# Staggering the addresses of a kernel's weight slots and operand arrays modulo 512 bytes

## What is computed

```python
h = layer_norm(ALPHA * h + y, ln_g[i, 0], ln_b[i, 0])       # y: the mixer's output
u = jnp.square(jax.nn.relu(h @ w_up[i])) @ w_down[i]        # 1024 -> 4096 -> 1024
h = layer_norm(ALPHA * h + u, ln_g[i, 1], ln_b[i, 1])
h = h + jax.nn.sigmoid(h @ w_ple_gate[i]) * (p[i] @ w_ple[i])
```

## Time and profile before

| | |
|---|---|
| median of three runs | 3551.2 us |
| span of the profiled execution | 3552.2 us |
| matmuls | 18416 |
| of these 512 columns wide, lines 497 to 499 | 11328 |
| of these 256 columns wide, lines 530 to 532 and 618 to 620 | 4704 |
| TensorE (PE) busy | 99% |
| VectorE (DVE) / ScalarE (ACT) / GpSimd (POOL) busy | 50% / 27% / 18% |
| mean granted TensorE clock | 0.998 |

### The profile page before, as it was taken

The page is one execution under the profiler, slowest core; times in us unless marked ns, Lnnn a source line. Parts: engine busy times, 40 slices in busy tenths (PEclk is TensorE's granted clock), DMA queues, the critical chain, the costliest instruction groups (busy, mean ns, idle before and its releaser), DMA issues.

```text
span 3552.2 us, 44299 instructions
## 1 busy us (share of the span) xinstructions
PE 3512.9 (99%) x18416; PEld 2952.0 (83%) x18416; DVE 1766.9 (50%) x2276; ACT 960.4 (27%) x1679; POOL 632.3 (18%) x372
## 2 busy tenths in 40 slices
PE   9999999999999999999999999999999999999999
PEld 7788888889888888688888878888888888898887
DVE  5454334556653346763336445553474346563434
ACT  3562001334220013630013256210141215120102
POOL 2112111200131112031112111311121111211110
PEclk9999999999999999999999999999999999999999
DMA  5322222222222223122222221222222222322222
GB/s 205 107 78 90 95 95 92 104 85 85 70 100 95 95 83 111 59 89 95 95 95 95 101 84 72 98 95 95 83 77 102 72 95 95 107 95 95 95 95 71
DMA packets 65463, 332.88 MB, mean 94 GB/s; under 512 B 9795, under 2 KB 20291, under 8 KB 28532
## 3 DMA queue, kind: packets, MB, share of 16 engines
q1 hardware_dynamic: 44316, 303.50, 23.8%
q10 hardware_dynamic: 20952, 26.56, 2.3%
HBM read 326.22 MB, written 10.90 MB: 95 GB/s over the span
## 4 chain that ended last, share of the span: by engine, by line
PE 88%; DVE 6%; ACT 4%; issue 1%; POOL 1%; DMA 0%; DVEq 0%; ACTq 0%; POOLq 0%
PE proj L497 23%; PE proj L499 23%; PE proj L498 23%; PE proj L618 2%; PE proj L619 2%; PE proj L620 2%; PE proj L530 2%; PE proj L532 2%; PE proj L531 2%; DVE wlo L1767 1%; PE mix L708 1%; DVE s L1877 1%; ACT xh L1182 1%; ACT h L1185 1%; PE mix L734 1%
## 5 line engine op out<-in xcount | busy, mean ns | idle before, releaser
L467 POOL TENSOR_SCALAR whi<-raw 128x2048 fp32r<-128x2048 f32 x272 | 528.8, 1944 | 2689.9 <-DVE wlo L1767 1722.1
L497 PE MATMUL proj<-gh,whi 128*128 128x512 f32 x1952 | 777.6, 398 | 2.2 <-DVE wlo L1767 2.2
L499 PE MATMUL proj<-gh,wlo 128*128 128x512 f32 x1952 | 763.5, 391 | 0.0
L498 PE MATMUL proj<-gl,whi 128*128 128x512 f32 x1952 | 762.8, 391 | 0.0
L1767 DVE TENSOR_TENSOR wlo<-raw,whi 128x2048 fp32r<-128x2048 f32 x285 | 651.3, 2285 | 137.9 <-POOL whi L467 95.2
L497 PE MATMUL proj<-xh,whi 128*128 128x512 f32 x1760 | 695.4, 395 | 8.9 <-DVE wlo L1767 3.1
L498 PE MATMUL proj<-xl,whi 128*128 128x512 f32 x1760 | 688.5, 391 | 0.0
L499 PE MATMUL proj<-xh,wlo 128*128 128x512 f32 x1760 | 688.4, 391 | 0.0
L497 PEld LDWEIGHTS proj<-gh,whi 128*128 128x128 f32 x1952 | 367.0, 188 | 95.1 <-issue 15.6
L499 PEld LDWEIGHTS proj<-gh,wlo 128*128 128x128 f32 x1952 | 366.9, 188 | 80.0
L498 PEld LDWEIGHTS proj<-gl,whi 128*128 128x128 f32 x1952 | 367.1, 188 | 77.7 <-issue 1.9
(11 more groups left out here) (321 smaller groups left out, 4324.0 us busy)
## 6 DMA issues: line engine op xcount, KB each, us to landing
raw<-in_stream SPq DMA_DIRECT2D x286, 1024.0 KB, 4.8
da_b<-bias_da ACTq DMA_DIRECT2D x16, 512.0 KB, 3.4
bias_da<-bias_rows ACTq DMA_DIRECT2D x8, 512.0 KB, 8.8
h<-in_x ACTq DMA_DIRECT2D x4, 512.0 KB, 8.9
bias_sw<-bias_table ACTq DMA_DIRECT2D x1, 2048.0 KB, 9.9
pf<-in_p ACTq DMA_DIRECT2D x4, 512.0 KB, 6.8
sw_b<-bias_sw ACTq DMA_DIRECT2D x4, 512.0 KB, 3.6
out_features<-fin SPq DMA_DIRECT2D x8, 256.0 KB, 2.5
```

The lines of the kernel that those rows point to most:

```text
L467: nc.gpsimd.tensor_scalar(whi[SLOT[n]][:, :, :], raw[SLOT[n]][:, :, :], 1.0, 0.0, ALU.mult, ALU.add).then_inc(hi_done, 1)
L497: nc.tensor.matmul(out, wh, ah, start=first, stop=False, skip_group_check=check)
L498: nc.tensor.matmul(out, wh, al, start=False, stop=False, skip_group_check=check)
L499: return nc.tensor.matmul(out, wl, ah, start=False, stop=last, skip_group_check=check)
```

## The change

Each weight slot and each of the four arrays gets a start modulo 512 bytes of its own. `phase` moves the allocator forward to it. Slots 0 to 3 start at 128, 160, 192 and 224; `xh` at 128, `xl` at 256, `gh` at 384, `gl` at 0. Nothing else is edited; instructions, their order, waits and transfers stay.

```diff
+SLOT_PHASE = (128, 160, 192, 224)
+MOVING_PHASE = {"xh": 128, "xl": 256, "gh": 384, "gl": 0}
...
+        def phase(offset):
+            top[0] += (offset - top[0]) % 512
+
         for i in range(3):
+            phase(SLOT_PHASE[i])
             place_slot(i)
         h = place("h", [P, KT, S])
+        phase(MOVING_PHASE["xh"])
         hg_m = place("hg_m", [P, 2, S], at=top[0] + 6 * S * 4)
         xh = place("xh", [P, KT, S], F32R)
+        phase(MOVING_PHASE["xl"])
         pick = place("pick", [P, len(HG_LEVELS), 2, P // 2], I32, at=top[0] + 6 * S * 4)
         xl = place("xl", [P, KT, S], F32R)
+        phase(MOVING_PHASE["gh"])
         gh = place("gh", [P, KT, S], F32R)
+        phase(MOVING_PHASE["gl"])
         gl = place("gl", [P, KT, S], F32R)
...
         small = place("small", [P, 256])
+        phase(SLOT_PHASE[3])
         fourth = top[0]
         place_slot(3)
```

## The result

The changed kernel takes 3589.57 us, the median of four runs (3588.02 to 3590.82), beside 3551.43 us for the kernel before in the same runs: 1.0103 times as long, with a 95% interval of 1.0089 to 1.0116. It is slower, as forecast, and inside the range, but by 38 us where 15 were forecast.

What follows compares the result with a forecast made beforehand. TensorE was taken as the bound, busy 99% at top clock, so the cost per matmul decides. Terms 9.7 (x) + 10.1 (g) - 4.5 (256 columns) gave +15.3 us, 3566 us; range 3508 to 3604 us.

Steps and rivals of the forecast that it cites:

- The reading of slot 3 and of the "ple" rows: 512-column matmuls: price follows moving-to-stationary distance, not the slot: 226.7 ns at 0, 228.5 at +64, 233.4 at -64.
- the marks that the prediction set: Profile after: x units near 227 ns on slot 0, 232 on slot 2; narrow 117 to 118; g mean above 227.8.
- The narrow ones: 256-column matmuls, half units and moving weights: gain on slots 0 to 2, partly lost on slot 3; sum -4.5 us.
- the x term: 5280 matmuls with x arrays moving, priced slot by slot at their new distances: sum +9.7 us.
- for distances with no row I take the nearest ones: Pricing of unseen x distances: +128 and +96 as +64 (228.5 ns), -32 at 230.0, +32 at 227.6, -96 at 233.4.
- the g term: 5904 matmuls with g arrays moving, taken as 128 to 256 bytes from distance 0: sum +10.1 us.
- the mean of the three known prices, 229.5: Price in ns for every g matmul: +2.8 on slots 0 to 2, -3.9 on slot 3.
- the upper bound of the prediction: Slowest row, 233.4 ns, for every g matmul (+33 us) and for unseen x distances (some +20): together about +50 us.
- The counts of x matmuls by slot: Spread of the x matmuls used in the sum: 1296, 1248, 1500 and 1236 on slots 0 to 3.
- The far distances are good: Rival: surplus fades at 128 bytes or more, g matmuls at 220.0 ns; -41 us, 3510 us; faster given 0.30.
- No change: Rival: better and worse distances balance, or distance is not the cause; 3551 us, within 7 us; chance 0.12.
- worse than any seen: Rival: -64 is not the worst distance, and some of sixteen reach 240 ns or more; some 3600 us; chance 0.08.

## Why the prediction was wrong

**What held.** The bound: TensorE throughout, with the clock untouched and no new wait. The reading of slot 3 and of the "ple" rows: the distance moves the time of every 512-column matmul, 226.7 ns at 0 and more elsewhere. The narrow matmuls of the half units at about 118 ns instead of 120. The sign. By the marks that the prediction set, x units on slot 2 came near 232 ns (231.2) and the g units' mean above 227.8; x units on slot 0, forecast near 227, came to 229.1 or 233.4.

**What failed is the size of two terms of the sum.** x was forecast at +9.7 us and came to +15.1 by the busy times and +16.0 from start to start; g was forecast at +10.1 and came to +21.5 and +22.3. The narrow ones were forecast at -4.5 and came to -2.8 and -1.2: slots 0 to 2 gained, but token chunks on slot 3 lost, such as those near 181 us, from 117.8 to between 120 and 121 ns, where the sum had them unchanged. In the x term, "for distances with no row I take the nearest ones" put 128 and 96 at 228.5 ns and -32 halfway at 230.0. Alone in a unit they measured 232.4, 233.4 and 233.1. Nearness is no guide: 64 is at 229.1, between 48 and 80 at 233.2 and 231.1. In the g term, "the mean of the three known prices, 229.5" had the good price of 0 as one of three. Of the 24 distances tried alone, modulo 256, only 0 stood at 227 ns in every unit, apart from a few at the borders of stages, and 21 of the 24 had medians from 231.1 to 235.4; the others are 0, 64 at 229.1, and -16 with its three speeds. So an unseen distance should have been priced like the worse of the known ones, and the upper bound of the prediction, with the slowest row for every unseen distance and some +50 us, was nearer than its middle. The counts of x matmuls by slot are off as well: the order of the slabs gives 1248, 1296, 1536 and 1200 on slots 0 to 3, which moves the x term by some 0.2 us.

**What was wrong without harm.** The distances are eight, not sixteen, and the g arrays are not far from the slots. A matmul has no price of its own distance: with more than one distance in a unit, or at -16, it depends on the rhythm that the unit takes over. The two partly cancel in a total; the history alone is worth 8 us, as the swap of two slots shows.

**The rivals.** "The far distances are good" falls: no distance of the g arrays was under 227 ns. "No change" falls with 1.0103. Of "worse than any seen" only the first half came: -64 is not the worst distance, and 20 of the 191 full units of the changed kernel stand at 235.5 ns. None of these is at 240, and the longest step that whole units kept to in any run is the 236.7 ns of distance -16.

**What stays open.** That the stationary load and the moving read meet at some place with a period of 256 bytes is argued from the dependence on their distance, not shown. Why there are several rhythms, why -16 has three where 0, -32, -64 and -96, alone in a unit, kept to one each within a run, and which load it is that meets the stream, the runs don't tell.

## What to carry to other kernels

Where TensorE streams float32r matmuls back to back, compare the start-to-start time of one shape in different buffers before changing anything else; a buffer that is some 3% off can be a matter of its address. Here the cure was the opposite of staggering: weight slots and moving arrays at equal addresses modulo 256 bytes gave the shortest 512-column step, and aligning the one slot that was off gained 0.35%. A table of prices read from a few neighbours should not be continued to others, and where one configuration shows two times, look at what ran before it.

## What the runs showed of the hardware that I had not expected

- The period of 256 bytes: with the x arrays moved by 256, slots 2 and 0 took 11.20 and 10.9 us as before, equal to within 0.01 us.
- Several steady speeds for the same instructions at the same addresses: at distance -16, 226.7 and 236.4 ns in one kernel, 233.3 and 236.7 in another; 231.1 and 235.5 ns on slot 3 of the changed kernel. At -16 they last through hundreds of matmuls; in the changed kernel they repeat every eight units.
- The two widths want different distances: at distance 0, 226.7 ns for 512 columns and 120.0 for 256; at -16 everywhere, 233.3 to 236.7 and 117.2.
- The smallest surplus over one column a cycle of a whole unit stayed 226.7 - 213.3 = 13.4 ns at 512 columns, whatever the layout. The Trainium skill ("TensorE: Matmul & The Clock Gate", Back-to-back issue gap) gives columns / 2.4 + 2.5 ns, which would be 215.8 ns, for a single matmul's gap; no unit here came near it.
